# Six mixed projection stages with their ring order changed from pairs to dense, modulation, modulation, dense

## The chip, the cores and the metric

The kernel runs on one core of one Trainium2 chip. The metric is the device time of one execution in microseconds, as the median of several runs. All stages belong to one launch.

## The reference

A residual stream `x` of 256 tokens by 2048 features passes through a state-space block, an attention block and then a second pair of mixers with a feed-forward part. All numbers are float32. Only the first part bears on the change:

```
c_act = silu(c)
shift, scale, gate = split(c_act @ mod_w[0] + mod_b[0], 3)      # 2048 x 6144
h = rmsnorm(x) * (1 + scale) + shift
u, z = split(h @ w_in)                                          # 2048 x 4096
y = gelu(diagonal state-space scan of u)
y = y * sigmoid(y @ w_glu + b_glu)
x = x + gate * ((y * silu(z)) @ w_out)
kv_shift, kv_scale = split(c_act @ kv_mod_w + kv_mod_b)
h_kv = modulated rmsnorm(x);  kv = h_kv @ w_kv;  small compression MLP
h = modulated rmsnorm(x);     q = h @ w_q
```

Two kinds of products stand beside each other. A dense product multiplies 256 token columns by a weight matrix. A modulation product multiplies one single vector, `c_act`, by a matrix that is just as large.

## The kernel before

Weights come through a ring of four slots in on-chip memory (`ring`, RING = 4), each 2 MB: 2048 rows by 256 columns. Each slot also has a PSUM bank of the same number (`bank[s]`), where the products of a dense tile in that slot go. Tile number n of the whole early program lies in slot n % 4. The early program is `ORDER`: `mod0` (16 modulation tiles), `u`, `z`, `glu`, `out`, `kv` (16 tiles each), `kvrow` (4 dense), `cmp` (2), and `q` (16).

The six stages in `MIXED` (`u`, `z`, `glu`, `out`, `kv`, `q`) hold 8 dense and 8 modulation tiles each. `place` gives the ring place of a dense tile, `mod_slots` those of a pair of modulation tiles, and `stream_mixed` issues the loads on SyncE's queue in one fixed order. `load` waits until the slot's earlier tile has been freed (`wait_free`), and since there is one queue, a load that waits holds back every load behind it. In `u`, `z` and `glu` the order is dense, dense, modulation, modulation; in `out`, `kv` and `q` (`MODS_FIRST`) it is modulation, modulation, dense, dense.

Who uses a slot and frees it:

- A dense tile: TensorE runs 32 matmuls (`dense`, L286), then ScalarE takes the two result tiles out of the bank and frees the slot (`drain_to` L420, `act_glu` L1375, `act_residual` L496).
- A pair of modulation tiles in `u`, `glu`, `out`, `kv`, `q`: VectorE multiplies both by `c_act` in 16 steps (`mod_pair`, L354 once and L356 fifteen times), frees both slots, and TensorE folds the sums into columns (`mod_columns`, L371). `dense` runs the fold of pair m after dense tile 2m+2, that of the last pair after the last tile.
- A modulation tile of `z`: TensorE multiplies it itself (`mod_rows`, L394) between pieces of the scan (`pe_ssm`), and ScalarE copies the row out of `bank[3]` (L1221).

`pe_ssm` interleaves, for 16 turns b, the scan's products with half a dense tile of `z` (L316): the outputs of turn b-1 (from L1249 on), the inputs of turn b+1 (L1235), the half tile and, in even turns, the row product of one modulation tile. ScalarE frees dense tile m and row m in the odd turn 2m+1.

`dve_glu` runs after `dve_mods(dve, "glu")`. It waits until the last dense tile of `glu` has been drained (`wait_drained`) and multiplies the whole gated unit in four pieces of 1024 columns (L1387). TensorE waits for all four:

```
            dense(pe, "glu", u_all)
            pe.wait_ge(glu_ready, 4)
            pe_residual(pe, "out", tiles(B(2)))
```

GpSimd makes the other factor, `gelu(y) * silu(z)`, in one product over 4096 columns (`pool_glu`, L1393) at the start of `glu`. In `out`, `dve_residual` alternates a modulation pair with two residual tiles. `dve_norm1` runs the norm for `kv`, the pairs of `kv`, then the norm for `q`. SyncE loads `x` a second time between the streams of `glu` and `out` (L2765).

After `q` the late ring takes over (`zc` and all that follows), which uses three slots and is not touched.

Of the kernel before, what the change touches and what calls it, by code (L numbers as in the profile page):

```python
# [23 lines left out]
ALU = mybir.AluOpType  # L24
# [10 lines left out]
RING = 4  # L35
# [67 lines left out]
SPLIT_INDEX = {x: m for m, x in enumerate(SPLITS)}  # L103
ACTED = ("zc", "ga", "gb", "gb2")
ACT_BASE = {n: sum(len(SPLIT[m]) for m in ACTED[:k]) for k, n in enumerate(ACTED)}

MODS_FIRST = ("out", "kv", "q")

TURNS = {n: 4 * k for k, n in enumerate(m for m in MIXED if m not in ROWS)}

# [1 line left out]
def build(nc, t):  # L112
    ctx = ExitStack()
    with ctx:
# [32 lines left out]
        def B(k, lo=0, n=4096):  # L147
            return arena[:, 4096 * k + lo:4096 * k + lo + n]
# [73 lines left out]
        def stream_mixed(sp, name, src, mod_src):  # L222
            with sp.Fori(0, COUNT[name] // 8) as i:
                def rows(p):
                    for x, (n, r) in enumerate(mod_slots(name, i, p)):
                        load(sp, n, r, mod_src(i, 2 * PAIRS[name] + 2 * p + x))

                for p in range(2):
                    if name in MODS_FIRST:
                        rows(p)  # L230
                    for k in (2 * p, 2 * p + 1):
                        n, r = place(name, i, k)
                        load(sp, n, r, src(i, k))
                    if name not in MODS_FIRST:
                        rows(p)

        def tiles_of(name, count=SLOT):

# [19 lines left out]

        def place(name, i, k):

            late = 2 if name in MODS_FIRST else 0
            return (BASE[name] + k + k // 2 * 2 + late, 2 * i) if name in MIXED else (BASE[name] + k, i)

        def mod_slots(name, i, k):

            late = 0 if name in MODS_FIRST else 2
            return [(BASE[name] + 4 * k + late + x, 2 * i) for x in range(2)]

        def slot_ready(pe, name, i, k):
            n, r = place(name, i, k)  # L270
# [5 lines left out]
        def dense(pe, name, act, kd=KD, ready=None):  # L276


            def body(i, k):
                s = slot_ready(pe, name, i, k)  # L280
                w = ring[:, s, :].rearrange("p (j n) -> p j n", n=SLOT_COLS)
                for f in range(2):
                    for j in range(kd):
                        if ready and k == 0 and f == 0 and j % QUARTER == 0:
                            pe.wait_ge(ready[0], ready[1] + j // QUARTER + 1)
                        last = nc.tensor.matmul(bank[s][:, T * f:T * f + T], w[:, j, P * f:P * f + P], act[:, j, :],  # L286
                                                start=j == 0, stop=j == kd - 1)
                last.then_inc(products, 1)
            if name not in TURNS:
                steps(pe, name, body)  # L290
                return

            pairs = DENSE[name] // 2
            for m in range(DENSE[name]):
                body(m // 4, m % 4)
                if m % 2 == 0 and m:
                    mod_columns(pe, name, (m // 2 - 1) // 2, (m // 2 - 1) % 2)
            mod_columns(pe, name, (pairs - 1) // 2, (pairs - 1) % 2)
# [42 lines left out]
        def mod_pair(dve, name, i, k):  # L341

            slots, acc = mod_slots(name, i, k), ACC[name]

            dve.wait_ge(acc_used, 2 * i + TURNS[name] + k + 1)
            for n, r in slots:
                wait_landed(dve, n, r)
            s0, s1 = (n % RING for n, _ in slots)
            for j in range(KD):
                at = slice(SLOT_COLS * j, SLOT_COLS * j + SLOT_COLS)  # L350

                w, a = ring[:, s0:s1 + 1, at], acc[:, k % 2]
                if j == 0:
                    nc.vector.tensor_scalar(a, w, c_act[:, j:j + 1], None, ALU.mult)  # L354
                else:
                    nc.vector.scalar_tensor_tensor(a, w, c_act[:, j:j + 1], a, ALU.mult, ALU.add)  # L356
                if j < KD - 1:
                    dve.drain()
            dve.drain().then_inc(acc_ready, 1)
            for s in (s0, s1):  # L360
                nc.vector.nop().then_inc(slot_free[s], 1)
# [60 lines left out]
            steps(act, name, body)  # L422

        def wait_drained(eng, name):
            n = BASE[name] + COUNT[name] - (3 if name in MIXED and name not in MODS_FIRST else 1)

            eng.wait_ge(slot_free[n % RING], n // RING + 2)

# [43 lines left out]
        SUMS = {"out": 1, "o": 2, "out2": 3}  # L472
        sum_ready = sem("sum_ready")

        def pe_residual(pe, name, act):

            dense(pe, name, act)
            pe.wait_ge(sum_ready, 8 * SUMS[name])
            for n in range(1 if SQUARES[name][2] is None else 2):
                for f in range(2):  # L480
                    last = nc.tensor.matmul(A(n, 0, T), ones[:], sq_sum[n][:, T * f:T * f + T], start=f == 0, stop=f == 1)
            last.then_inc(ms_ready, 1)
# [709 lines left out]
        def z_place(b):  # L1192
# [3 lines left out]
            n, r = place("z", i, k)  # L1196
            return i, k, n, m, *row_place(m)

        def row_place(m):

            return BASE["z"] + 4 * (m % 4 // 2) + 2 + m % 2, 2 * (m // 4)

        def act_ssm(act):
            def finish(b):
                act.wait_ge(ysum_ready, b + 1)
                nc.scalar.activation(u_all[:, b, :], u_all[:, b, :], ACT.Gelu_apprx_tanh).then_inc(y_kept, 1)

            for b in range(SBLOCKS):
                if b + 1 < SBLOCKS:
                    act_trig(act, b + 1)  # L1210
                if b:
                    finish(b - 1)
                if b % 2:

                    i, k, n, m, row, turn = z_place(b)
                    s = product_ready(act, "z", i, k)
                    nc.scalar.copy(z_all[:, 2 * m:2 * m + 2, :],
                                   bank[s][:].rearrange("p (f n) -> p f n", f=2)).then_inc(slot_free[s], 1)
                    act.wait_ge(rows_ready_m, COUNT["mod0"] + m + 1)
                    act.wait_ge(cols_ready, COUNT["mod0"] + m)  # L1220
                    nc.scalar.copy(rstd[:], bank[3][:, 0:SLOT_COLS]).then_inc(slot_free[row % RING], 1)  # L1221
            finish(SBLOCKS - 1)
            act.drain()
            nc.scalar.activation(B(1), B(1), ACT.Silu).then_inc(z_kept, 1)

        def pe_ssm(pe):
# [35 lines left out]
            for b in range(SBLOCKS):  # L1262
                if b:
                    outputs(b - 1)
                if b + 1 < SBLOCKS:
                    inputs(b + 1)
                i, k, n, m, row, turn = z_place(b)
                if b % 2 == 0:
                    slot_ready(pe, "z", i, k)
                dense_piece(n % RING, hT, KD * (b % 2), KD)  # L1270
                if b % 2 == 0:

                    if m:
                        old, old_turn = row_place(m - 1)
                        wait_free(pe, old + RING, old_turn)
                        mod_row_columns(rstd[:], bank[3][:, 256 + 2 * m - 2:256 + 2 * m])
                    wait_landed(pe, row, turn)
                    wait_free(pe, row, turn)
                    mod_rows(row, bank[3][:, 0:SLOT_COLS])
            outputs(SBLOCKS - 1)  # L1280
            wait_free(pe, row + RING, turn)
            mod_row_columns(rstd[:], bank[3][:, 256 + 14:256 + 16])

        def dve_turns(dve, b):
            dve.wait_ge(turns_ready, b + 1)
# [44 lines left out]
        def dve_z_bias(dve):  # L1330
            dve.wait_ge(cols_ready, COUNT["mod0"] + 8)
            at = 4 * PAIRS["z"]
            nc.vector.tensor_tensor(mod[:, at:at + 16], bank[3][:, 256:272], col("mod_b", at, 16), ALU.add)
            dve.drain()

        def pool_ssm(pool):
# [43 lines left out]

        def dve_glu(dve):

            dve_z_bias(dve)
            wait_drained(dve, "glu")
            dve.wait_ge(yz_ready, 1)
            for q in range(4):
                nc.vector.tensor_tensor(B(2, 1024 * q, 1024), B(2, 1024 * q, 1024), B(1, 1024 * q, 1024),  # L1387
                                        ALU.mult).then_inc(glu_ready, 1)

        def pool_glu(pool):  # L1390
            pool.wait_ge(y_kept, SBLOCKS)
# [1404 lines left out]
        def _(pe):  # L2796
            pe_mean_square(pe, B(2))
            pe_mod0(pe)
            dense(pe, "u", hT, ready=(h_ready, 0))
            pe_ssm(pe)  # L2800
            pe.wait_ge(y_kept, SBLOCKS)
            dense(pe, "glu", u_all)
            pe.wait_ge(glu_ready, 4)
            pe_residual(pe, "out", tiles(B(2)))
            dense(pe, "kv", tiles(B(0)), ready=(h_ready, 4))
            dense_rows(pe, "kvrow", tiles(B(0)))
            pe_cmp(pe)
            dense(pe, "q", hT, ready=(h_ready, 8))
            pe_gates(pe)
            for s in range(LCOUNT["zc"]):  # L2810
                late_split(pe, "zc", s, h_quarters, zc_halves, (ZC_H, ZC_H))
# [130 lines left out]
        def _(dve):  # L2942
# [8 lines left out]
            dve_turns(dve, 0)  # L2951
            dve_mods(dve, "u")
            dve_ssm(dve)
            dve_mods(dve, "glu")
            dve_glu(dve)
            dve.wait_ge(x_again, 16)
            dve_residual(dve, "out", tiles(B(3)), GT0)
# [164 lines left out]
```

## Time and profile before

| | |
|---|---|
| median of 3 runs | 3289.23 us (3289.2 to 3289.51) |
| profiled execution | 3291.9 us, span 3289.8 us |
| TensorE matmul busy | 3160.6 us, 96% |
| VectorE busy | 1723.0 us, 52% |
| mean DMA rate | 182 GB/s |
| granted TensorE clock, mean | 0.984 |

The span counts from the first instruction of the program to the last. TensorE is busy nearly all the time, so what counts is where it stops. The stages of the change lie between 110 us and 1024 us of the span: `u` to 231, the scan with `z` to 439, `glu` to 567, `out` to 703, `kv` to 831, `kvrow` and `cmp` to 902, `q` to 1024.

### The profile page before, as it was taken

The numbers are of one execution on the slowest core, as the hardware profiler recorded it, in microseconds if no ns is written. First come the engines' busy times: TensorE is split into PE (matmuls) and PEld (weight loads), VectorE is DVE, ScalarE is ACT, GpSimd is POOL, SyncE is SP. The second block draws the span as 40 slices with busy tenths as digits, with TensorE's granted clock in tenths as the row PEclk, the third lists the DMA queues.
The fourth block names the chain that finished last, engine by engine and source line by source line (L and its number), as shares of the span: only waits on it lengthen the run. The fifth ranks groups of instructions, "written<-read, shape, count | busy, mean of one in ns | idle before, by whom it ended". The sixth has DMA issues, their size and how long they took to land.

```text
span 3289.8 us, 54033 instructions
## 1 busy us (share of the span) xinstructions
PE 3160.6 (96%) x22938; PEld 2877.1 (87%) x22938; DVE 1723.0 (52%) x2641; ACT 453.8 (14%) x801; POOL 139.8 (4%) x89
## 2 busy tenths in 40 slices
PE   5999998989999999999999999999999999999999
PEld 3787787878888988889888888889999999999999
DVE  5357635344244333465545764576666555555443
ACT  2104420000001133221310012211010000000000
POOL 0003310000000000012000000000010000000000
PEclk8999998999999999999999999999999999999999
DMA  9763457657474423234335442333544444444443
GB/s 410 325 281 129 180 231 306 275 205 303 170 289 164 175 107 120 111 128 154 128 131 189 155 147 102 116 145 121 190 165 161 172 169 163 178 156 170 160 168 138
DMA packets 51016, 599.37 MB, mean 182 GB/s; under 512 B 9535, under 2 KB 12190, under 8 KB 13342
## 3 DMA queue, kind: packets, MB, share of 16 engines
q1 hardware_dynamic: 50846, 596.88, 47.1%
q8 instruction: 134, 2.20, 0.3%
q14 instruction: 36, 0.29, 0.0%
HBM read 593.70 MB, written 3.16 MB: 181 GB/s over the span
## 4 chain that ended last, share of the span: by engine, by line
PE 84%; DMA 8%; DVE 5%; DVEq 1%; issue 1%; ACT 0%; SPq 0%; POOLq 0%; POOL 0%; ACTq 0%
PE bank L2600 24%; PE bank L741 18%; PE bank L792 16%; PE bank L286 10%; DMA ring<-in_t_mod 7%; PE bank L316 3%; DVE E L356 3%; PE bank L738 2%; PE bank L328 2%; PE bank L394 1%; PE bank L567 1%; PE aux L1608 1%; PE bank L557 1%; PE aux L1655 1%; DMA ring<-in_t_kv 1%
## 5 line engine op out<-in xcount | busy, mean ns | idle before, releaser
L741 PE MATMUL bank<-hT,ring 128*128 128x256 f32 x2496 | 552.5, 380 | 0.0
L741 PEld LDWEIGHTS bank<-hT,ring 128*128 128x128 f32 x2496 | 470.8, 190 | 76.6 <-issue 15.3
L2600 PE MATMUL bank<-arena,ring 128*128 128x128 f32 x3440 | 396.4, 275 | 0.0
L2600 PEld LDWEIGHTS bank<-arena,ring 128*128 128x128 f32 x3440 | 390.2, 192 | 0.0
L286 PE MATMUL bank<-arena,ring 128*128 128x256 f32 x1536 | 343.6, 386 | 29.9 <-DMA ring<-in_t_kv 9.3
L286 PEld LDWEIGHTS bank<-arena,ring 128*128 128x128 f32 x1536 | 296.8, 194 | 73.1 <-issue 14.7
L792 PE MATMUL bank<-hT,ring 128*128 128x128 f32 x2624 | 320.4, 277 | 7.8 <-DVEq L847 5.8
L792 PEld LDWEIGHTS bank<-hT,ring 128*128 128x128 f32 x2624 | 305.7, 193 | 13.4 <-issue 7.2
L286 PE MATMUL bank<-hT,ring 128*128 128x256 f32 x1024 | 228.6, 386 | 8.7 <-DMA ring<-in_t_q 4.4
L286 PEld LDWEIGHTS bank<-hT,ring 128*128 128x128 f32 x1024 | 197.4, 194 | 37.2 <-DMA ring<-in_t_q 5.1
L2600 PE MATMUL bank<-hT,ring 128*128 128x128 f32 x1680 | 197.9, 275 | 0.0
L356 DVE SCALAR_TENSOR_TENSOR E<-ring,c_act,E 128x512 f32<-128x512 f32 x240 | 183.4, 764 | 18.5 <-issue 0.6
L2600 PEld LDWEIGHTS bank<-hT,ring 128*128 128x128 f32 x1680 | 192.7, 192 | 0.1
L792 PE MATMUL bank<-arena,ring 128*128 128x128 f32 x1472 | 175.6, 275 | 1.9 <-DVEq L606 1.5
L792 PEld LDWEIGHTS bank<-arena,ring 128*128 128x128 f32 x1472 | 170.1, 192 | 2.6 <-issue 1.9
L2691 DVE TENSOR_TENSOR arena<-bank,w_gate 128x256 f32<-128x256 f32 x50 | 21.2, 425 | 203.8 <-ACT rstd L2639 132.4
L2600 PE MATMUL bank<-arena,E 128*128 128x128 f32 x1024 | 119.7, 275 | 0.0
L2600 PEld LDWEIGHTS bank<-arena,E 128*128 128x128 f32 x1024 | 117.0, 192 | 0.0
L316 PE MATMUL bank<-hT,ring 128*128 128x256 f32 x512 | 116.5, 386 | 0.0
L316 PEld LDWEIGHTS bank<-hT,ring 128*128 128x128 f32 x512 | 97.2, 192 | 15.0 <-issue 0.4
L2097 DVE TENSOR_TENSOR W<-E,arena 128x128 f32<-128x128 f32 (+7 forms) x64 | 74.9, 1170 | 44.9 <-issue 27.8
L354 DVE TENSOR_SCALAR E<-ring,c_act 128x512 f32<-128x512 f32 x16 | 7.8, 486 | 168.3 <-DMA ring<-in_t_mod 166.4
(438 smaller groups left out, 3649.0 us busy)
## 6 DMA issues: line engine op xcount, KB each, us to landing
ring<-in_t_mod SPq DMA_DIRECT2D x64, 2048.0 KB, 13.6
ring<-in_t_gu SPq DMA_DIRECT2D x44, 2048.0 KB, 8.3
ring<-in_t_out SPq DMA_DIRECT2D x16, 2048.0 KB, 8.5
ring<-in_t_zs SPq DMA_DIRECT2D x16, 2048.0 KB, 8.3
ring<-in_t_down SPq DMA_DIRECT2D x16, 2048.0 KB, 7.3
ring<-in_t_gdn SPq DMA_DIRECT2D x12, 2048.0 KB, 8.3
ring<-in_t_u SPq DMA_DIRECT2D x8, 2048.0 KB, 8.9
ring<-in_t_z SPq DMA_DIRECT2D x8, 2048.0 KB, 8.4
```

What stands on the lines that cost most here:

```text
L286: last = nc.tensor.matmul(bank[s][:, T * f:T * f + T], w[:, j, P * f:P * f + P], act[:, j, :], start=j == 0, stop=j == kd - 1)
L316: last = nc.tensor.matmul(bank[s][:, T * f:T * f + T], w[:, j, P * f:P * f + P], act[:, j, :], start=j == 0, stop=j == KD - 1)
L328: last = nc.tensor.matmul(bank[s][:, T * f:T * f + T], act[:, j, P * f:P * f + P], w[:, j, :], start=j == 0, stop=j == KD - 1)
L356: nc.vector.scalar_tensor_tensor(a, w, c_act[:, j:j + 1], a, ALU.mult, ALU.add)
L394: last = nc.tensor.matmul(out[32 * q:32 * q + 32, :], c_act[:, j:j + 1].to_broadcast([P, 32]), w[:, j, :], start=a == 0, stop=a == KD // 4 ...
L557: last = nc.tensor.matmul(out[:, T * f:T * f + T], w[:, j, P * f:P * f + P], x[:, j, :], start=j == 0 and f == 0, stop=j == KD - 1 and f == 1)
L567: last = nc.tensor.matmul(out[:, T * f:T * f + T], w[:, j, P * f:P * f + P], x[:, j, :], start=j == 0, stop=j == KD - 1)
L738: last = nc.tensor.matmul(out[:, T * f:T * f + T], act[:, j, P * f:P * f + P], w[:, j, :], start=j == 0, stop=j == kd - 1)
L741: last = nc.tensor.matmul(out[:, T * f:T * f + T], w[:, j, P * f:P * f + P], act[:, j, :], start=j == 0, stop=j == kd - 1)
L792: last = nc.tensor.matmul(out[:, P * at:P * at + P], a[:, j, :], tile_at(b, j), start=j == 0 and q in (0, 3), stop=j == half - 1 and q in ...
L2097: v.tensor_tensor(tmp, Tsol[:, :, 0:J], row, ALU.mult)
L2600: last = nc.tensor.matmul(out[:, P * q:P * q + P], a[:, j, :], b[:, j, :], start=begins and q == 0 and j == 0, stop=ends and q == len(grou ...
```

## The change

All six mixed stages use one order: dense, modulation, modulation, dense. `MODS_FIRST` goes. In `u` to `kv` the dense tiles thus lie in slots 0 and 3 and the modulation tiles in slots 1 and 2. `q` begins in slot 2, so its dense tiles lie in slots 2 and 1 and its modulation pair in slots 0 and 3, which `mod_pair` reads with a stride of three slots. The row products of `z` move from `bank[3]` to `bank[1]`. The gated unit is multiplied tile by tile: `dve_glu` alternates one modulation pair with two products of 512 columns, each as soon as ScalarE has drained that tile, and the first dense tile of `out` waits for them piece by piece (every two feature tiles) and not for all at its start.

```diff
@@ stream_mixed
                 for p in range(2):
-                    if name in MODS_FIRST:
-                        rows(p)
                     for k in (2 * p, 2 * p + 1):
                         n, r = place(name, i, k)
                         load(sp, n, r, src(i, k))
-                    if name not in MODS_FIRST:
-                        rows(p)
+                        if k % 2 == 0:
+                            rows(p)
@@ place, mod_slots
-            late = 2 if name in MODS_FIRST else 0
-            return (BASE[name] + k + k // 2 * 2 + late, 2 * i) if name in MIXED else (BASE[name] + k, i)
+            return (BASE[name] + 4 * (k // 2) + 3 * (k % 2), 2 * i) if name in MIXED else (BASE[name] + k, i)
-            late = 0 if name in MODS_FIRST else 2
-            return [(BASE[name] + 4 * k + late + x, 2 * i) for x in range(2)]
+            return [(BASE[name] + 4 * k + (2 - x if name == "q" else 1 + x), 2 * i) for x in range(2)]
@@ dense
-                        if ready and k == 0 and f == 0 and j % QUARTER == 0:
-                            pe.wait_ge(ready[0], ready[1] + j // QUARTER + 1)
+                        if ready and k == 0 and f == 0 and j % ready[2] == 0:
+                            pe.wait_ge(ready[0], ready[1] + j // ready[2] + 1)
@@ mod_pair
-                w, a = ring[:, s0:s1 + 1, at], acc[:, k % 2]
+                w, a = ring[:, s0:s1 + 1:s1 - s0, at], acc[:, k % 2]
@@ row_place
-            return BASE["z"] + 4 * (m % 4 // 2) + 2 + m % 2, 2 * (m // 4)
+            return BASE["z"] + 4 * (m % 4 // 2) + 1 + m % 2, 2 * (m // 4)
@@ act_ssm, pe_ssm, dve_z_bias: bank[3] becomes z_rows = bank[1][:]
@@ dve_glu
-            dve_z_bias(dve)
-            wait_drained(dve, "glu")
-            dve.wait_ge(yz_ready, 1)
-            for q in range(4):
-                nc.vector.tensor_tensor(B(2, 1024 * q, 1024), B(2, 1024 * q, 1024), B(1, 1024 * q, 1024),
+            for s in range(DENSE["glu"]):
+                if s % 2 == 0:
+                    mod_pair(dve, "glu", s // 4, s // 2 % 2)
+                if s == 0:
+                    dve_z_bias(dve)
+                    dve.wait_ge(yz_ready, 1)
+                n, r = place("glu", s // 4, s % 4)
+                dve.wait_ge(slot_free[n % RING], r + n // RING + 2)
+                nc.vector.tensor_tensor(B(2, 512 * s, 512), B(2, 512 * s, 512), B(1, 512 * s, 512),
                                         ALU.mult).then_inc(glu_ready, 1)
+            dve_mod_bias(dve, "glu")
@@ the program of TensorE
-            pe.wait_ge(glu_ready, 4)
-            pe_residual(pe, "out", tiles(B(2)))
+            pe_residual(pe, "out", tiles(B(2)), (glu_ready, 0, 2))
```

The other calls of `dense` name their step (QUARTER), which is what they had. `wait_drained` no longer needs to tell the two orders apart.

## Rows read from the trace of the kernel before

**Rows 1.** The page's chain by engine, and TensorE's waits over the whole span: total, times, longest.

```profile
PE 84%; DMA 8%; DVE 5%; DVEq 1%; issue 1%; ACT 0%; SPq 0%; POOLq 0%; POOL 0%; ACTq 0%
PE bank L394 <- DMA ring<-in_t_mod: 29.7, 17, 3.9
PE aux L371 <- DVEq L359: 7.7, 2, 4.2
```

**Rows 2.** Windows of `out`: stretch, length, TensorE busy, granted clock, DMA share, GB/s.

```profile
567.50:584.10 16.60, 16.55 (x66) 0.86 0.53 209
584.10:598.00 13.90, 13.90 (x66) 1.00 0.68 292
```

**Rows 3.** Timeline at the end of `u`: start, length, instruction, idle before.

```profile
211.98 14.06 PE L286 MATMUL bank<-hT,ring 128*128 128x256 f32 x64
229.61 1.05 PE L371 MATMUL aux<-ones,E 128*128 128x1 f32 x8 [3.57 <-DVEq L359]
```

**Rows 4.** Timeline of the scan: outputs of turns 3, 5, 7 and 13 begin.

```profile
281.87 0.42 PE L1249 MATMUL bank<-arena,E 32*32 32x128 f32 x8
...
309.91 0.42 PE L1249 MATMUL bank<-arena,E 32*32 32x128 f32 x8
...
332.98 0.42 PE L1249 MATMUL bank<-arena,E 32*32 32x128 f32 x8
...
414.12 0.42 PE L1249 MATMUL bank<-arena,E 32*32 32x128 f32 x8
```

**Rows 5.** Timeline of SyncE's queue in the scan: loads issued.

```profile
260.09 22.99 SPq L213 DMA_DIRECT2D ring<-in_t_z  x2
283.27 0.86 SPq L213 DMA_DIRECT2D ring<-in_t_mod  x2
```

**Rows 6.** Three loads issued from 614.4 us on within 1.1 us: issue to landing.

```profile
DMA to landing us min/median/max: 8.2/12.6/16.9
```

**Rows 7.** One load issued at 599.0 us with nothing before it: issue to landing.

```profile
DMA to landing us min/median/max: 8.2/8.2/8.2
```

**Rows 8.** Timeline of `glu` and the start of `out`, all engines.

```profile
437.48 1.35 SPq L213 DMA_DIRECT2D ring<-in_t_mod  x2
...
439.44 41.71 PE L286 MATMUL bank<-arena,ring 128*128 128x256 f32 x192 [0.51 <-ACT arena L1206]
...
444.50 8.84 POOL L1393 TENSOR_TENSOR arena<-arena 128x4096 f32<-128x4096 f32 x1 [11.24 <-ACT arena L1224]
...
455.08 0.49 DVE L354 TENSOR_SCALAR E<-ring,c_act 128x512 f32<-128x512 f32 x1 [16.14 <-DMA ring<-in_t_mod]
455.64 12.31 DVE L356 SCALAR_TENSOR_TENSOR E<-ring,c_act,E 128x512 f32<-128x512 f32 x15
456.05 12.86 SPq L213 DMA_DIRECT2D ring<-in_t_glu  x2
...
538.83 14.06 PE L286 MATMUL bank<-arena,ring 128*128 128x256 f32 x64
...
557.05 1.86 PE L371 MATMUL aux<-ones,E 128*128 128x1 f32 x8 [4.16 <-DVEq L359]
...
567.55 44.00 PE L286 MATMUL bank<-arena,ring 128*128 128x256 f32 x192 [8.64 <-issue]
```

**Rows 9.** Timeline of the scan: GpSimd and VectorE at once, and VectorE alone.

```profile
240.72 1.26 POOL L1349 TENSOR_TENSOR E<-E,xT 128x512 f32<-128x512 f32 x1 [4.26 <-DVE xT L1286]
240.74 1.80 DVE L1325 TENSOR_TENSOR xT<-xT,W 128x512 f32<-128x512 f32 x1
...
429.52 0.68 DVE L1325 TENSOR_TENSOR xT<-xT,W 128x512 f32<-128x512 f32 x1
```

**Rows 10.** Timeline of `out`, `kv` and `q`: each stage's third dense tile.

```profile
632.43 16.38 PE L286 MATMUL bank<-arena,ring 128*128 128x256 f32 x64 [6.17 <-DMA ring<-in_t_out]
...
743.41 15.51 PE L286 MATMUL bank<-arena,ring 128*128 128x256 f32 x64 [9.30 <-DMA ring<-in_t_kv]
...
935.19 16.88 PE L286 MATMUL bank<-hT,ring 128*128 128x256 f32 x64 [4.35 <-DMA ring<-in_t_q]
```

More of the change, by code:

```diff
@@ L105 @@
 ACT_BASE = {n: sum(len(SPLIT[m]) for m in ACTED[:k]) for k, n in enumerate(ACTED)}
-MODS_FIRST = ("out", "kv", "q")
 TURNS = {n: 4 * k for k, n in enumerate(m for m in MIXED if m not in ROWS)}
@@ L424, in wait_drained @@
         def wait_drained(eng, name):
-            n = BASE[name] + COUNT[name] - (3 if name in MIXED and name not in MODS_FIRST else 1)
+            n = BASE[name] + COUNT[name] - 1
             eng.wait_ge(slot_free[n % RING], n // RING + 2)
@@ L473, in build, with pe_residual @@
         sum_ready = sem("sum_ready")
-        def pe_residual(pe, name, act):
-            dense(pe, name, act)
+        def pe_residual(pe, name, act, ready):
+            dense(pe, name, act, ready=ready)
             pe.wait_ge(sum_ready, 8 * SUMS[name])
@@ L1197, in z_place @@
             return i, k, n, m, *row_place(m)
+        z_rows = bank[1][:]
         def row_place(m):
-            return BASE["z"] + 4 * (m % 4 // 2) + 2 + m % 2, 2 * (m // 4)
+            return BASE["z"] + 4 * (m % 4 // 2) + 1 + m % 2, 2 * (m // 4)
         def act_ssm(act):
@@ L1220, in act_ssm @@
                     act.wait_ge(cols_ready, COUNT["mod0"] + m)
-                    nc.scalar.copy(rstd[:], bank[3][:, 0:SLOT_COLS]).then_inc(slot_free[row % RING], 1)
+                    nc.scalar.copy(rstd[:], z_rows[:, 0:SLOT_COLS]).then_inc(slot_free[row % RING], 1)
             finish(SBLOCKS - 1)
@@ L1275, in pe_ssm @@
                         wait_free(pe, old + RING, old_turn)
-                        mod_row_columns(rstd[:], bank[3][:, 256 + 2 * m - 2:256 + 2 * m])
+                        mod_row_columns(rstd[:], z_rows[:, 256 + 2 * m - 2:256 + 2 * m])
                     wait_landed(pe, row, turn)
                     wait_free(pe, row, turn)
-                    mod_rows(row, bank[3][:, 0:SLOT_COLS])
+                    mod_rows(row, z_rows[:, 0:SLOT_COLS])
             outputs(SBLOCKS - 1)
             wait_free(pe, row + RING, turn)
-            mod_row_columns(rstd[:], bank[3][:, 256 + 14:256 + 16])
+            mod_row_columns(rstd[:], z_rows[:, 256 + 14:256 + 16])
         def dve_turns(dve, b):
@@ L1332, in dve_z_bias @@
             at = 4 * PAIRS["z"]
-            nc.vector.tensor_tensor(mod[:, at:at + 16], bank[3][:, 256:272], col("mod_b", at, 16), ALU.add)
+            nc.vector.tensor_tensor(mod[:, at:at + 16], z_rows[:, 256:272], col("mod_b", at, 16), ALU.add)
             dve.drain()
@@ L2798, in _ @@
             pe_mod0(pe)
-            dense(pe, "u", hT, ready=(h_ready, 0))
+            dense(pe, "u", hT, ready=(h_ready, 0, QUARTER))
             pe_ssm(pe)
@@ L2802, in _ @@
             dense(pe, "glu", u_all)
-            pe.wait_ge(glu_ready, 4)
-            pe_residual(pe, "out", tiles(B(2)))
-            dense(pe, "kv", tiles(B(0)), ready=(h_ready, 4))
+            pe_residual(pe, "out", tiles(B(2)), (glu_ready, 0, 2))
+            dense(pe, "kv", tiles(B(0)), ready=(h_ready, 4, QUARTER))
             dense_rows(pe, "kvrow", tiles(B(0)))
             pe_cmp(pe)
-            dense(pe, "q", hT, ready=(h_ready, 8))
+            dense(pe, "q", hT, ready=(h_ready, 8, QUARTER))
             pe_gates(pe)
@@ L2953, in _ @@
             dve_ssm(dve)
-            dve_mods(dve, "glu")
             dve_glu(dve)
```

## The prediction

> **What bounds the kernel now.** I read the page's chain first, then TensorE's waits, then the timeline of each mixed stage. The chain gives TensorE 84% of the span and transfers 8% [rows 1], and with 96% busy TensorE is the bound; a gain must come from its stops before 1024 us. The reader is to see that the stops are few, long, and lie at fixed places of the ring order: rows of `z` waiting for modulation tiles, the last fold of a stage waiting for VectorE [rows 1], the third dense tile of `out`, `kv` and `q` waiting for its load [rows 10], and 8.64 us before `out`'s first tile, which only wait for the gated unit's product [rows 8]. A stop costs twice: the tile after it runs at a granted clock of 0.86, which mixes stretches at 1.2 GHz with 2.4 GHz, and takes 16.6 us where the next at 1.00 takes 13.9 [rows 2].
>
> **Two constants.** A 2 MB load alone lands 8.2 us after its issue [rows 7]. Three issued together land after 8.2, 12.6 and 16.9 us; with the 0.5 us between issues that is one every 4.9 us, in the order of issue [rows 6]. A modulation pair takes VectorE 0.49 + 12.31, with gaps 12.9 us, from landing to free slots [rows 8]. A dense tile takes 13.86 us and a fold 0.8, so two tiles with a fold take 28.5.
>
> **The change, place by place.** The same loads, matmuls and modulation steps are done. What moves is which load stands behind which in SyncE's one queue.
>
> *u.* Today the last pair of modulation tiles is loaded behind the last dense tile and multiplied after it: the last fold starts at 229.61, though the last tile, begun at 211.98, ends at 226.04 [rows 3]. Afterwards the last pair is issued ahead of the last dense tile, when the third pair frees its slots. Going through the stage with the constants: pair 0 starts at 119.5 (VectorE is free then, both tiles landed), pair 1 at 146, pair 2 at 173, pair 3 at 202, done by 215. The fold can follow tile 7 at once: 229.61 - 226.04 = **3.6 us**. The queue's other loads have margins: the second dense tile of a pair is issued when its predecessor is drained, lands behind the two modulation tiles, and is 4 us early. TensorE then idles less before the scan; that may spare it part of a slow stretch, at most some 3.7 us (two input groups and a half tile at half speed). I take nothing for it and keep the end.
>
> *z.* Modulation tile 2 is needed in turn 4. Today it is queued behind dense tile 3, whose slot comes free in turn 3: issued at 282.75 (260.09 + 22.99 less the issue), the modulation tile at 283.27 [rows 5], which lands too late. Outputs of turns 3 and 5 lie 28.04 us apart, those of 5 and 7, where the tile is there already, 23.07 [rows 4]. The pattern comes three times; from turn 3 to turn 13 there are five such intervals, three long: 132.25 - 5 x 23.07 = **16.9 us**. Afterwards dense tile 2 and modulation tile 2 go into slots 0 and 1, free in turn 1 (the load at 260.09 [rows 5]), and land by 273.4, 19 us early; tiles 3 are needed only in turn 6. VectorE, GpSimd and ScalarE keep up, since they do in the short intervals.
>
> *glu, the gain.* Today tile 7 starts at 538.83; with its fold that is 553.5, yet `out` begins at 567.55 [rows 8]. The last pair (4.16 us of stop) and then the four products stand in between. Afterwards pairs are done before tile 7 ends, and products 0 to 6 too; product 7, about 0.6 us, comes after ScalarE's 0.84, near 554.7. `out`'s first tile wants it only for its fourteenth matmul, 6 us on. So the wait is wholly covered: 567.55 - 553.54 = 14.0 us. The tile that ran slowly, 44.00 for three against 41.71 for three at the start of `glu` [rows 8], gives 2.3 more.
>
> *glu, the loss.* Pair 0 today starts at 455.08, behind both modulation tiles issued at 437.48 [rows 8]. Afterwards the first of them is loaded a turn pair earlier and the second lands near 445.4, so VectorE would start then, under GpSimd's 8.84 us product, begun at 444.50. Do they run together? A VectorE product of 0.68 us takes 1.80 beside GpSimd's and ends 0.56 us after it [rows 9]: it stood still until GpSimd was done. So the pair's fifteen long steps wait until 453.3 and end at 465.7. Modulation tiles 2 and 3 are issued at 466.0 and 466.5 and land at 474.2 and 479.1; dense tile 3, whose slot is free at 468.6 (456.05 + 12.86 less the issue [rows 8]), lands third, at 484.0. TensorE wants it at 481.8: 2.2 us of stop. No stop as short as this shows what the clock does after it; between nothing and the 2.8 us after a stop of 4.35 [rows 10] I take 1.0. If the two engines ran side by side the loss is 0. Net of `glu`: 14.0 + 2.3 - 3.2 = **13.1 us**.
> The Trainium skill (SBUF — State Buffer, Who interferes with whom) says that a VectorE operation with two inputs in SBUF and a GpSimd operation that reads SBUF exclude each other for a whole instruction, which speaks against this change. The trace agrees with it in the 1.80 us [rows 9]; without the lock the sum would be 3.2 us better.
>
> In `glu` VectorE's pairs now also wait for products, so for drained tiles. Pair 1 starts at 479.1 (landing), pair 2 at 505 (landing; product 3 is possible at 499), pair 3 at 532, done by 545; tile 7 ends at 555. Margin 10 us. The load of `x` has its slot after tile 7's load and lands 12 us ahead of its use.
>
> *out, kv, q.* Today dense tile 2 stands behind two modulation tiles, whose slots come free only when VectorE ends pair 0; the three go out together and the dense tile lands last, 16.9 us on [rows 6]. Afterwards dense tile 2 is ahead of them and goes out when tile 0 is drained, 8.2 us of load under a 13.9 us tile. `out` also loses its four modulation tiles in a row. Saved are the idle time and the slow tile against 14.06 [rows 8, 10]: `out` 6.17 + 2.32 = **8.5**, `kv` 9.30 + 1.45 = **10.8**, `q` 4.35 + 2.82 = **7.2 us**. Dense tile 3 now stands behind the pair. It is issued when tile 1 is drained, about 14 us before its use; the pair's loads are 7 to 11 us older, so it lands 4 to 5 us early in each of the three. In `q` pair 0 starts 4 us later than today (its slot 0 is `cmp`'s first), which its 12 us of margin at the first fold hides. The last fold of these stages stays behind tile 7, the strided read of slots 0 and 3 has the same 512 columns.
>
> **The sum.** 3.6 + 16.9 + 13.1 + 8.5 + 10.8 + 7.2 = 60.1 us. From the span of 3289.8 that leaves 3229.7. The profiled execution (3291.9) stands 2.1 above its span and 2.7 above the median, so I take the sum off the median: 3289.2 - 60.1 = **3229 us**. What follows `q` keeps its work and its loads.
>
> **Rivals.**
> 1. *The clock stays slow.* If the slow stretches come anyway, from TensorE's own pattern, the idle time goes and its 2.3, 2.3, 1.5 and 2.8 us stay, with some 5.8 in `z` (16.9 less three stops of up to 3.9): 3244 us. For it: slow stretches also lie where no load is late. Against it: tiles without a stop ahead run at 1.00 [rows 2].
> 2. *The scan's own chain takes over.* VectorE, GpSimd and ScalarE finish only about 1 us before the outputs in the short intervals; if they need the long ones to catch up, `z` gives nothing: 3246 us. Against it: the short intervals are equal to 0.01 us.
> 3. *VectorE's new order in `glu` binds.* If each later pair must wait for a drained tile and then for its loads, a cycle is 12.9 + 17.4 + some 1 = 31 us against 28.5, three times, and the last fold waits again: some 8 to 10 us back, 3239 us. The margin of 10 us must be used up first.
> 4. *The other side: the second dense tile of each pair comes late.* It stands behind two modulation tiles now. If VectorE ends a pair after the odd dense tile is drained, all three go out together and this one lands 17.3 us on with 13.9 there: 3.4 idle and about 2.2 of slow clock, 5.6 us a place. There are 15 such places (`u`, `glu`, `out`, `kv`, `q`, three each): 84 us, 3313 us. It decides from the eleventh place on. I find VectorE 7 to 11 us ahead everywhere but in `glu`'s first.
>
> **How the numbers follow.** Chances: the sum as worked out 0.70 (own range 3222 to 3236: the 3.7 us at the scan's start and the 3.2 of the lock below, one more stop like `glu`'s above), rival 1 0.09, rival 2 0.07, rival 3 0.10, rival 4 0.04. The likeliest gives 3229. The range goes from 3222 to rivals 1 and 3, 3245. 0.2%, 6.6 us, is about what a measurement of this kernel tells from no change. Faster 0.95; same 0.02 (rival 4 in about eleven places); slower 0.03.
>
> **What would show it.** Right: outputs of odd turns 23.1 us apart all through `z`; no stop before L394 from the scan on; `out`'s first tile within 1 us of `glu`'s last fold; no stop at the third dense tiles; pair 0 of `glu` stretched to some 20 us by L1393 and a stop of about 2 us before `glu`'s fourth tile. Wrong: stops at fourth, sixth or eighth dense tiles with a release by a dense load (rival 4), folds that wait for VectorE in `glu` (rival 3), or intervals over 24 us in `z` released by VectorE or GpSimd (rival 2). Wrong by more than the range it would be if `zc` began later than shifted, since its first load now waits until `q`'s seventh dense tile is drained from slot 2.

## The result

| | |
|---|---|
| before, median of 4 | 3289.37 us (3289.2 to 3290.47) |
| changed, median of 4 | 3229.68 us (3228.36 to 3233.59) |
| ratio of the times | 0.9818, 95% interval 0.9806 to 0.983 |
| profiled span, before and changed | 3289.8 and 3226.6 us |
| granted TensorE clock, mean | 0.984 and 0.992 |

The change makes the kernel 59.7 us faster, where 60.1 were forecast; 3229 us stood against 3229.7. The two profiled executions differ by more, 63.2 us of span: the one before was a long one (3291.9 us against a median of 3289.37), the changed one was the shortest of its four, which spread over 5 us. So the gains by stage below, read from these two, add up to 3.5 us more than the medians show.

The chain of the changed kernel's page, and some of TensorE's waits (total, times, longest), which answer to [rows 1]:

```profile
PE 93%; DMA 3%; DVE 2%; DVEq 1%; ACT 0%; issue 0%; SPq 0%; POOLq 0%; POOL 0%; ACTq 0%
```

```profile
PE bank L388 <- DMA ring<-in_t_mod: 19.5, 15, 3.2
...
PE bank L280 <- DVE arena L635: 5.7, 2, 5.3
...
PE bank L280 <- DMA ring<-in_t_glu: 2.1, 1, 2.1
```

Transfers fell from 8% of the chain to 3%. L388 (L394 before) now waits in `mod0` alone, 10 us less. Waits of `mod_columns` for VectorE, 7.7 us before, are not in the list. Of the dense loads only one of `glu` is still waited for; those of `out`, `kv` and `q` [rows 10] have gone.

Where the 63.2 us came from, by the start of each stage's first work on TensorE in the two profiled executions:

| stretch | before | after | gain | forecast |
|---|---|---|---|---|
| to the scan's first inputs (`u`) | 231.05 | 227.19 | 3.9 | 3.6 |
| scan with `z`, to `glu` | 208.39 | 190.62 | 17.8 | 16.9 |
| `glu`, to `out` | 128.11 | 116.32 | 11.8 | 10.8 |
| `out`, to `kv` | 136.16 | 124.68 | 11.5 | 10.8 |
| `kv`, `kvrow`, `cmp`, to `q` | 199.23 | 188.11 | 11.1 | 10.8 |
| `q`, to the end of its last tile | 120.88 | 113.45 | 7.4 | 7.2 |
| the rest | 2266.0 | 2266.2 | -0.2 | 0 |

The forecast of `glu` is 14.0 - 3.2; the 2.3 us of the slow tile after it belong to `out`'s row here. The end of `u` and the scan, against [rows 3, 4]:

```profile
211.96 14.06 PE L280 MATMUL bank<-hT,ring 128*128 128x256 f32 x64
...
225.86 0.95 PE L365 MATMUL aux<-ones,E 128*128 128x1 f32 x8
```

```profile
277.12 0.42 PE L1245 MATMUL bank<-arena,E 32*32 32x128 f32 x8
...
300.20 0.42 PE L1245 MATMUL bank<-arena,E 32*32 32x128 f32 x8
...
323.27 0.42 PE L1245 MATMUL bank<-arena,E 32*32 32x128 f32 x8
...
392.49 0.42 PE L1245 MATMUL bank<-arena,E 32*32 32x128 f32 x8
```

The last fold follows the last tile with no idle time noted. The outputs of turns 3, 5 and 7 stand 23.08 and 23.07 us apart; turn 13 comes 115.37 us after turn 3, five times 23.07. The long intervals are gone, and the scan's other engines (VectorE, ScalarE, GpSimd) keep up. The start of `glu`, which answers to [rows 8]:

```profile
417.81 41.71 PE L280 MATMUL bank<-arena,ring 128*128 128x256 f32 x192 [0.52 <-ACT arena L1202]
...
422.88 8.84 POOL L1394 TENSOR_TENSOR arena<-arena 128x4096 f32<-128x4096 f32 x1 [11.23 <-ACT arena L1220]
423.92 8.08 DVE L348 TENSOR_SCALAR E<-ring,c_act 128x512 f32<-128x512 f32 x1 [6.61 <-DMA ring<-in_t_mod]
432.07 12.31 DVE L350 SCALAR_TENSOR_TENSOR E<-ring,c_act,E 128x512 f32<-128x512 f32 x15
...
444.68 0.86 SPq L211 DMA_DIRECT2D ring<-in_t_mod  x2
...
446.94 14.15 SPq L211 DMA_DIRECT2D ring<-in_t_glu  x2
...
462.36 27.89 PE L280 MATMUL bank<-arena,ring 128*128 128x256 f32 x128 [2.06 <-DMA ring<-in_t_glu]
...
533.32 0.95 PE L365 MATMUL aux<-ones,E 128*128 128x1 f32 x8
...
534.13 41.04 PE L280 MATMUL bank<-arena,ring 128*128 128x256 f32 x189
534.59 0.69 DVE L1387 TENSOR_TENSOR arena<-arena 128x512 f32<-128x512 f32 x1 [9.39 <-ACT arena L1371]
```

VectorE's first step, 0.49 us long elsewhere, lasts 8.08: it begins 1.04 us after GpSimd's product and ends 0.28 us after it. The pair ends at 444.4, its followers go out at 444.68 and just after, the fourth tile's load at 446.94 stands behind them, and TensorE stops for 2.06 us. At the other end `out` begins 0.81 us after the start of the last fold, and the last product is made under its first matmuls.

### The profile page after: what moved, and what is told of

The parts are those of the page before. It is cut to its first block, busy times and chain, and to the rows that moved or that the text cites. A ratio compares the mean times of both kernels' runs of the same rounds, so it can differ in the third digit from the quotient of the medians.

```text
span 3226.6 us, 54024 instructions
## 1 busy us (share of the span) xinstructions
PE 3142.2 (97%) x22938; PEld 2866.8 (89%) x22938; DVE 1730.4 (54%) x2645; ACT 454.2 (14%) x801; POOL 139.3 (4%) x89
## 4 chain that ended last, share of the span: by engine, by line
PE 93%; DMA 3%; DVE 2%; DVEq 1%; ACT 0%; issue 0%; SPq 0%; POOLq 0%; POOL 0%; ACTq 0%
PE bank L2601 25%; PE bank L735 18%; PE bank L280 16%; PE bank L786 16%; PE bank L310 4%; DMA ring<-in_t_mod 3%; PE bank L732 2%; PE bank L322 2%; PE bank L561 1%; PE aux L1609 1%; PE bank L388 1%; PE bank L551 1%; PE aux L1656 1%; PE aux L1231 1%; PE bank L518 1%; PE bank L1249 0%
## 5 line engine op out<-in xcount | busy, mean ns | idle before, releaser
L735 PEld LDWEIGHTS bank<-hT,ring 128*128 128x128 f32 x2496 | 470.8, 190 | 76.6 <-issue 15.3
L280 PE MATMUL bank<-arena,ring 128*128 128x256 f32 x1536 | 336.6, 381 | 8.3 <-DVE arena L635 5.7
L1676 DVE TENSOR_TENSOR arena<-aux,con 128x60 f32<-128x60 f32 (+2 forms) x24 | 17.1, 712 | 129.7 <-PE aux L1609 129.7
```

Source lines behind the costliest of these rows:

```text
L735: last = nc.tensor.matmul(out[:, T * f:T * f + T], w[:, j, P * f:P * f + P], act[:, j, :], start=j == 0, stop=j == kd - 1)
```

## The experiments

Unless said otherwise, each is the changed kernel with the edit shown. The times of the kernel before beside them had medians from 3290.5 to 3291.6.

**z_queue_old.** The slots stay as changed, but `z`'s loads are issued in the old order.

```diff
-                        if k % 2 == 0:
+                        if k % 2 == (1 if name == "z" else 0):
                             rows(p)
```

> The changed kernel, with every tile in its new slot, but in z alone SyncE issues dense, dense, modulation, modulation as before. My theory (the stop in z is the queue's order and nothing else): modulation tiles 2, 4 and 6 wait again behind a dense tile that waits for its slot, three intervals of odd turns are about 28 to 29.7 us where the change has 23.07, and the time is 3229.7 + 16.9 = 3246.6 us. Rival (the new slots or banks are what helped z, not the order of issue): all intervals stay at 23.07 us and the time stays within 3 us of 3229.7.

Measured: 3246.68 us (3246.07 to 3247.7), ratio to before 0.9864 [0.9848, 0.9881]. Its outputs of turns 3, 5 and 7:

```profile
278.01 0.42 PE L1245 MATMUL bank<-arena,E 32*32 32x128 f32 x8
...
306.16 0.42 PE L1245 MATMUL bank<-arena,E 32*32 32x128 f32 x8
...
329.24 0.42 PE L1245 MATMUL bank<-arena,E 32*32 32x128 f32 x8
```

28.15 and 23.08 us apart: the long interval is back. The median is 17.0 us above the result's; in the trace the outputs of turn 13 come at 408.79, 130.78 us after turn 3, which is 15.4 us more than five short intervals. The other 1.6 us are not located. With banks and slots unchanged, the order of issue alone brings the stops back.

**u_queue_old.** The same edit with "u" for "z".

> The changed kernel, with every tile in its new slot, but in u alone SyncE issues dense, dense, modulation, modulation. My theory: the last modulation pair is loaded behind the last dense tile again, the last fold waits for VectorE until about 3.6 us after the last tile, and the time is 3.6 to 4 us more than the change, 3233.7 us. Rival (the scan's start is set by something else and the fold's 3.6 us are hidden): no change against 3229.8.

Measured: 3236.36 us (3235.02 to 3237.7), 0.9835 [0.9823, 0.9847], 6.4 us above change_again (below), where 3.6 to 4 were expected. Timeline at the end of `u`:

```profile
229.32 1.05 PE L365 MATMUL aux<-ones,E 128*128 128x1 f32 x8 [3.28 <-DVEq L353]
...
230.76 2.09 PE L1231 MATMUL aux<-arena 32*128 32x128 f32 x32 [0.39 <-DVEq L380]
```

The scan's first inputs come at 230.76 and not 227.19, the 3.6 us of the fold. They also run slowly, 2.09 us against 1.17 in the changed kernel, and `glu` starts 4.5 us later than in the first profile of the change (422.32 against 417.81), 3.6 later than in that of change_again (418.71). After its stop in `glu` two tiles take 30.75 us (467.28 to 498.03), the slow stretch described under change_again; but change_again has one as long, and its span is only 3.2 us shorter (3231.9 against 3235.1). So the traces show the fold's 3.6 us and up to 0.9 more at the scan's start. What makes the difference of the medians 6.4 us is not shown.

**residual_orders_alone.** The kernel before with the new order in three stages, the old products. `place`, `mod_slots` and `wait_drained` follow the same list.

```diff
+SPLIT_ORDER = ("out", "kv", "q", )
@@ stream_mixed
                 for p in range(2):
-                    if name in MODS_FIRST:
+                    if name in MODS_FIRST and name not in SPLIT_ORDER:
                         rows(p)
                     for k in (2 * p, 2 * p + 1):
                         n, r = place(name, i, k)
                         load(sp, n, r, src(i, k))
-                    if name not in MODS_FIRST:
+                        if k % 2 == 0 and name in SPLIT_ORDER:
+                            rows(p)
+                    if name not in MODS_FIRST and name not in SPLIT_ORDER:
                         rows(p)
```

> The kernel before with the new order in out, kv and q alone; u, z and glu keep dense, dense, modulation, modulation, and the products of the gated unit are the old ones. My theory: the stops at the third dense tiles go (8.5 + 10.8 + 7.2 = 26.5 us), and out's first tile, whose load no longer stands behind glu's last modulation pair, starts when the last of the four products is done at about 564.3 instead of 567.55, 3.2 us more: 3289.4 - 29.7 = 3259.7 us. Rival (a stop that goes here comes back at a later tile, because the second dense tile of each pair now stands behind two modulation tiles): stops of 3 us or more at fourth, sixth or eighth tiles and a gain under 20 us, 3270 us or more.

Measured: 3260.46 us (3260.14 to 3261.82), 0.9906 [0.9889, 0.9922], against 3259.7 expected. Against the kernel before beside it (3291.57) that is 31.1 us, where 29.7 were expected. TensorE waits for no dense load in `out`, `kv` or `q`. Slots and order were changed together here; only in `z` and `u` were they separated. `out` begins at 563.11, on the products:

```profile
558.42 4.63 DVE L1399 TENSOR_TENSOR arena<-arena 128x1024 f32<-128x1024 f32 x4
563.11 12.17 PE L295 MATMUL bank<-arena,ring 128*128 128x256 f32 x41 [5.30 <-DVE arena L1399]
```

**products_alone.** The kernel before in its old order, with the changed `dve_glu` and the stepwise wait.

```diff
-            dense(pe, "glu", u_all)
-            pe.wait_ge(glu_ready, 4)
-            pe_residual(pe, "out", tiles(B(2)))
+            dense(pe, "glu", u_all)
+            pe_residual(pe, "out", tiles(B(2)), (glu_ready, 0, 2))
@@ dve_glu
-            wait_drained(dve, "glu")
-            dve.wait_ge(yz_ready, 1)
-            for q in range(4):
+            for s in range(DENSE["glu"]):
+                if s % 2 == 0:
+                    mod_pair(dve, "glu", s // 4, s // 2 % 2)
...
```

> The kernel before in its old ring order, with the gated unit multiplied tile by tile and out's first tile waiting piece by piece. Theory A, formed after the result: in the old order out's first dense tile lies in a slot that glu's last modulation pair frees at 557.0, is issued at 557.3 and lands at 567.46, just before the tile started at 567.55; so the product was not the only thing in the way and the products alone give nothing: 3289.4 us, within 1.5. Theory B, the way the prediction put it (the last pair and then the four products stand in between): out starts at 558.0, 9.5 us earlier, 3280 us.

Measured: 3290.84 us (3287.87 to 3291.57), 0.9997 [0.9987, 1.0007]. No gain that can be told from none, as theory A said. The timeline shows what stands there instead:

```profile
558.16 1.63 PE L380 MATMUL aux<-ones,E 128*128 128x1 f32 x8 [4.36 <-DVEq L368]
558.37 0.86 SPq L216 DMA_DIRECT2D ring<-in_t_out  x2
558.39 1.29 DVE L1403 TENSOR_TENSOR arena<-arena 128x512 f32<-128x512 f32 x2 [0.31 <-issue]
...
568.26 6.90 PE L295 MATMUL bank<-arena,ring 128*128 128x256 f32 x22 [8.47 <-DMA ring<-in_t_out]
```

The products are done at 559.7. The tile is issued only at 558.37, when the last modulation pair gives up its slots, and TensorE waits 8.47 us for it. In the kernel before, the 8.64 us [rows 8] are set down to no releaser. Its timeline has both, the issue of `out`'s first loads and the products:

```profile
557.26 0.86 SPq L213 DMA_DIRECT2D ring<-in_t_out  x2
...
559.52 4.63 DVE L1387 TENSOR_TENSOR arena<-arena 128x1024 f32<-128x1024 f32 x4
```

The first of the two loads lands 10.2 us after its issue. Two waits ended there within 4 us of each other, the products at 564.2 and the first load at 567.5, and the later one hid the earlier.

**order_old_products.** The four old products, all awaited.

```diff
-            for s in range(DENSE["glu"]):
-                ...
+            wait_drained(dve, "glu")
+            dve.wait_ge(yz_ready, 1)
+            for q in range(4):
+                nc.vector.tensor_tensor(B(2, 1024 * q, 1024), B(2, 1024 * q, 1024), B(1, 1024 * q, 1024),
+                                        ALU.mult).then_inc(glu_ready, 1)
@@ the program of TensorE
+            pe.wait_ge(glu_ready, 4)
```

> The changed kernel with the four old products of 1024 columns after all of glu's tiles, all awaited by out's first tile. The load of that tile landed long before. Theory A: the fold ends at 534.1, ScalarE's last tile at 534.6, biases and four products take until about 540, so TensorE stops about 6 us and runs the next tile some 2.3 us longer at a lower clock: 3229.7 + 8 = 3238 us. Theory B (the load was the whole of the old stop and the products hide): 3230 us. With products_alone this tells how the 14 us between glu and out divide.

Measured: 3239.07 us (3237.58 to 3239.89), 0.9841 [0.9824, 0.9857].

```profile
537.29 4.63 DVE L1383 TENSOR_TENSOR arena<-arena 128x1024 f32<-128x1024 f32 x4
...
541.98 18.35 PE L280 MATMUL bank<-arena,ring 128*128 128x256 f32 x74 [5.30 <-DVE arena L1383]
```

The stop is 5.30 us and ends with the products. The three tiles after it take 43.82 us, where 41.69 is the time without a slow stretch. So the new products are worth some 9 us in the median, but only after the new order has brought the load forward.

**change_again.** The changed kernel, unedited, beside factor_on_vector and the two kv_pairs kernels. u_queue_old and factor_after_pair ran on another chip, so where they are set against it, differences of about 1 us mean little.

> The changed kernel itself once more, to stand on the same chip beside the three that follow: 3229.7 us, within 4, since its four runs so far lay between 3228.4 and 3233.6.

Measured: 3229.93 us (3229.06 to 3233.69), 0.9816 [0.9802, 0.9829]. Its profiled execution has a span of 3231.9, 5.3 us more than the first profile of the same kernel. Windows of it and of the first profile over the first 13.9 us after `glu`'s stop (stretch, length, busy PE, PEld, DVE, ACT, POOL, granted clock, DMA share, GB/s):

```profile
463.60:477.50 13.90, 13.89 (x50) 11.73 (x51) 8.11 (x11) 0.00 (x0) 0.00 (x0) 0.78 0.66 255
```

```profile
462.36:476.30 13.94, 13.94 (x65) 12.28 (x66) 8.10 (x11) 0.00 (x0) 0.00 (x0) 1.00 0.67 261
```

The clock fell to 0.78 here, a stretch at 1.2 GHz in it, and not in the first profile: 50 matmul records against 65 (the trace has 64 records for a tile's 32 matmuls). `glu` to `out` lasts 119.71 us against 116.32, which is 3.4 of the 5.3 us between the two spans. Seven of the profiled executions have the same code in this place:

| kernel | stop | clock of the next 13.9 us | next two tiles |
|---|---|---|---|
| changed, first profile | 2.06 | 1.00 | 27.89 |
| z_queue_old | 2.32 | 0.88 | 29.58 |
| kv_pairs_plus4 | 2.34 | 0.89 | 29.33 |
| change_again | 2.41 | 0.78 | 30.94 |
| u_queue_old | 2.46 | 0.79 | 30.75 |
| kv_pairs_plus8 | 2.52 | 0.88 | 29.58 |
| order_old_products | 2.73 | 0.88 | 29.58 |

Six of the seven have a slow stretch, which costs 1.4 to 3.1 us; the first profile of the change is the exception.

**factor_on_vector.** GpSimd's product is made by VectorE after the first pair, and `pool_glu` is gone.

```diff
                 if s == 0:
                     dve_z_bias(dve)
-                    dve.wait_ge(yz_ready, 1)
+                    dve.wait_ge(z_kept, 1)
+                    for q in range(4):
+                        nc.vector.tensor_tensor(B(1, 1024 * q, 1024), B(1, 1024 * q, 1024), B(0, 1024 * q, 1024), ALU.mult)
+                    dve.drain()
```

> The changed kernel with gelu(y) * silu(z) made by VectorE in four pieces of 1024 columns after glu's first modulation pair, and not by GpSimd beside it. My theory (GpSimd's 8.84 us product held the pair up and so made glu's fourth dense tile late): the pair lasts 12.9 us instead of 20.8, its followers are issued 8 us earlier, the fourth tile lands about 3 us before its use, TensorE's stop of 2.06 us goes, and the time is 2 us less than that of the change run beside it, 3227.6 us. Rival (the fourth tile is late because it is behind two modulation tiles in any case): the stop stays at 2 us and the time does not move.

Measured: 3228.98 us (3227.6 to 3229.1), 0.9813 [0.9799, 0.9826].

```profile
423.44 0.49 DVE L348 TENSOR_SCALAR E<-ring,c_act 128x512 f32<-128x512 f32 x1 [6.42 <-DMA ring<-in_t_mod]
424.00 12.31 DVE L350 SCALAR_TENSOR_TENSOR E<-ring,c_act,E 128x512 f32<-128x512 f32 x15
...
436.61 0.89 SPq L211 DMA_DIRECT2D ring<-in_t_mod  x2
...
459.87 20.32 PE L280 MATMUL bank<-arena,ring 128*128 128x256 f32 x93
```

The pair takes 12.87 us, the modulation tiles go out 8 us earlier, the fourth tile starts with no stop. The median moved by 1.0 us only, not 2, and the intervals overlap, so a gain is not shown; but the five times now lie within 1.5 us, where the change's five lie within 4.6. A stop of 2 us or more and the slow stretch after it are gone from the trace; why the median shows so little of that is open.

**factor_after_pair.** GpSimd keeps its product and starts it after the first pair.

```diff
             pool.wait_ge(z_kept, 1)
+            pool.wait_ge(acc_ready, TURNS["glu"] + 1)
             nc.gpsimd.tensor_tensor(B(1), B(1), B(0), ALU.mult).then_inc(yz_ready, 1)
```

> The changed kernel with GpSimd's product of 4096 columns kept where it is, but begun only when VectorE has done glu's first modulation pair. My theory (the two engines exclude each other for whole instructions; the one that waits should be GpSimd): pair 0 lasts 12.9 us, the product runs from about 437 to 446 us while VectorE waits anyway, the stop before glu's fourth tile goes, and with it the slow stretch of clock that follows it in some runs; time and spread as in factor_on_vector, 3227.5 to 3229.2 us in all five runs. Rival (what helped in factor_on_vector was that GpSimd did nothing): pair 0 short but the stop of about 2 us remains.

Measured: 3228.52 us (3227.91 to 3230.42), 0.9812 [0.98, 0.9824].

```profile
424.75 12.32 DVE L350 SCALAR_TENSOR_TENSOR E<-ring,c_act,E 128x512 f32<-128x512 f32 x15
...
437.26 8.84 POOL L1395 TENSOR_TENSOR arena<-arena 128x4096 f32<-128x4096 f32 x1 [25.47 <-DVEq L353]
```

VectorE's first step takes 0.49 us again. GpSimd works as long as before and the stop is gone all the same, so it was the overlap and not the work. Five of the six times lie within 0.9 us, one stands 1.7 above them. This is the version that I would keep: one line, about 1.4 us under the change in the medians, though the intervals do not separate the two.

**kv_pairs_plus4** and **kv_pairs_plus8.** VectorE's pairs of `kv` get longer, by eight steps as shown or by four.

```diff
             s0, s1 = (n % RING for n, _ in slots)
+            for _ in range(8 if name in ("kv", ) else 0):
+                nc.vector.scalar_tensor_tensor(acc[:, k % 2], ring[:, s0:s1 + 1:s1 - s0, 0:SLOT_COLS], c_act[:, 0:1],
+                                               acc[:, k % 2], ALU.mult, ALU.add)
+                dve.drain()
```

> The changed kernel with each of kv's four modulation pairs made about 3.3 us longer by four more VectorE steps whose results are overwritten. From the landings of the changed kernel: the fourth, sixth and eighth dense tiles still land 0.5 to 2 us before their use, so TensorE doesn't stop: 3229.7 us, within 1.5 of the change. Rival (each extra us of VectorE shows, the pairs set the pace): 13 us more, 3243 us.

> The same with eight more steps, 6.6 us a pair. The prediction's rival 4 put to the test: the second dense tile of each pair goes out with or behind the two modulation tiles. Going through the stage: the fourth tile stops TensorE 1.3 us, the sixth and the eighth about 4.3 each, and the last fold waits about 1 us: 10.9 us, with slow clock after the stops 11 to 16 us, so 3241 to 3246 us. If the prediction's margin of 7 to 11 us a pair were right as it stood, 6.6 us would cost nothing.

Measured: with four 3235.27 us (3231.69 to 3236.87), 0.9832 [0.9817, 0.9847]; with eight 3245.22 us (3240.9 to 3247.01), 0.9861 [0.9846, 0.9876]. The eighth tile with four steps:

```profile
765.16 14.08 PE L280 MATMUL bank<-arena,ring 128*128 128x256 f32 x64 [0.55 <-DMA ring<-in_t_kv]
```

The fourth, sixth and eighth with eight:

```profile
707.69 27.89 PE L280 MATMUL bank<-arena,ring 128*128 128x256 f32 x128 [1.36 <-DMA ring<-in_t_kv]
...
740.78 29.49 PE L280 MATMUL bank<-arena,ring 128*128 128x256 f32 x128 [4.41 <-DMA ring<-in_t_kv]
...
773.76 15.77 PE L280 MATMUL bank<-arena,ring 128*128 128x256 f32 x64 [2.71 <-DMA ring<-in_t_kv]
```

With eight the stops come at the tiles where they were expected, 1.36, 4.41 and 2.71 us (1.3 and twice 4.3 were worked out, and about 1 at the last fold, which does not wait), with a slow tile after each of the last two; `kv`'s dense tiles take 128.85 us (661.33 to 790.18) against 116.60, and 15.3 us are lost in the median. With four there is one stop, of 0.55 us, where none was expected, and `kv`'s dense tiles take 117.75 us, only 1.2 more; yet the median lies 5.3 us above the change. The profiled execution, whose span of 3232.0 is that of change_again, doesn't show the difference; whether the other executions had a slow stretch after the short stop is open. So "within 1.5" was missed, and "13 us more" too.

## Why the prediction was right

*u.* The fold's wait went as worked out: 3.9 us up to the first inputs instead of 3.6, and u_queue_old loses 3.6 there. The slow stretch at the scan's start was put at nothing, with an end of 3.7. From the first inputs to the first outputs it was 17.3 us before, 16.4 in the first profile of the change and 17.3 again in change_again. So the 0.9 us by which `z`'s row in the table stands above its forecast vary from execution to execution, and are not shown to come from the change.

*z.* Right to 0.1 us: 23.07 us in all five intervals, and z_queue_old loses 15.4 us in the trace and 17.0 in the median. Rival 2, the scan's own chain, didn't come.

*glu, the gain.* The sum was right, but the step that names what stood between `glu` and `out` was incomplete. It had "the last pair (4.16 us of stop) and then the four products". The load of `out`'s first tile, held back by the last modulation pair, ended last, as products_alone shows. The forecast survived because the change removes all three. That part of the number was luck: had only the products been changed, the same reasoning would have foretold 9.5 us, and 0.7 were measured, less than the noise.

*glu, the loss.* The overlap of the pair with GpSimd cost what was worked out: the pair ended 20.5 us after its start (20.3 forecast), the stop was 2.06 us (2.2 forecast). The slow clock was taken at 1.0 us between 0 and 2.8. It was nothing in the profiled execution and 1.4 to 3.1 us in six others, so the 1.0 was too low for most. That it makes the spread of the changed kernel is likely, since the two kernels without the stop spread less, but executions without a profile can't show it. Stop and slow stretch together are 2.1 to 5.5 us in the seven traces, but taking the overlap away moved the medians by only 1.0 and 1.4 us, within their intervals; so the net price of 3.2 us is not confirmed.

*out, kv, q.* Right to 0.7 us in each, and residual_orders_alone, which has these three and 3.2 us before `out`, came within 0.8 us of its forecast time and within 1.4 us of its forecast gain. In `out`'s row 0.4 us come from the norm's sums, 1.66 us instead of 2.07; in change_again they take 2.07 again, so these are not the change's.

*Rival 4.* Its mechanism exists: the second dense tile of each pair is late as soon as VectorE is. The margin that spoke against it was misjudged. "VectorE 7 to 11 us ahead" counts from one pair's end to one tile's drain, but a longer pair also delays its followers' loads, and so the next pair; three pairs in a row use the margin three times (so argued from the order of the queue; the sizes are measured). 3.3 us a pair are enough for a first stop, 6.6 cost 12 us in one stage.

## What to carry over

A single queue that feeds two consumers should put next the load whose consumer comes free next; a load behind one that waits for a slow consumer's slot pays that consumer's time, and the order of issue alone was worth 15 to 17 us in one stage. Where several waits end together, list when each of them is over: taking one away gives only the distance to the next, here nothing measurable alone and 9 us after the order was mended. When work moves to an engine's earlier idle time, look at what its neighbour did there: here a single wait on GpSimd's side takes the stop away again, though the gain in time is too small to be told from none.

## What the runs showed of the hardware

A VectorE TENSOR_SCALAR with one tensor input in on-chip memory, 0.49 us alone, stood still until GpSimd's 8.84 us product was done: it is 8.08 us long in the first profile of the change, 7.97 to 8.15 us in the six others with the overlap, and 0.49 us in the two kernels without it. I had expected this of the steps with two inputs and not of the first one. The Trainium skill (SBUF — State Buffer, Who interferes with whom) counts `tensor_scalar` among the operations that can enter a two-port mode and are then shut out by a GpSimd instruction that began first, for its whole length. The trace agrees: begun 1.04 us after GpSimd, done 0.28 us after it. And short stops of TensorE at one place, 2.06 to 2.73 us in seven profiled executions, were followed by a stretch at 1.2 GHz in six of them (granted clock 0.78 to 0.89 over the next 13.9 us, two tiles in 29.3 to 30.9 us) and by none in one (1.00, 27.9 us, after the stop of 2.06). The longest stop was not followed by the greatest loss: 29.58 us after 2.73, 30.94 after 2.41.
